# First stage of a streaming encoder step: low-rank columns on three 32-column strips, key products in another order, two value tiles ahead of the norm

## The chip, the core and the metric

The kernel runs on one core of a Trainium2 chip. The metric is the device time of one execution in microseconds (us). Engines are named as the profile names them: PE is TensorE, DVE is VectorE, ACT is ScalarE, POOL is GpSimd, SP is SyncE; PEld is TensorE's weight load, and a q behind a name (SPq, ACTq) is the issue of a DMA on that engine's queue.

## The reference, cut to what matters

The reference is one step of two layers over 1024 prompt frames and 64 sample frames of width 1024. The change lies in the beginning of the even layer, where the frames are normed and projected:

```python
h = _rmsnorm(x, norm_g)                       # x * rsqrt(mean(x*x) + eps) * g
z = h @ w_in
aq, ak, av, bq, bk, bv, blr, gate = _split(z, SPLIT_EVEN)
...                                           # ak, av: 256 columns each, blr: 16 columns
glog = jax.nn.log_sigmoid((blr @ w_lr + b_lr).astype(jnp.float32)) / B_GATE_NORM
```

The keys `ak` and values `av` go into sliding-window attention, `blr` gives the forget gates of four heads of gated linear attention. All is float32.

## The kernel before

Activations lie transposed, 8 blocks of 128 features by 1092 tokens (1024 + 64, padded), and a matmul takes a third of the tokens (364 columns; `NCH` = 3 of them). Weights come in pieces of 128x1024 in a fixed order: piece 0 the low-rank columns (16 real ones in a block of 128), 1 and 2 the keys (`PC_K`), 3 and 4 the values (`PC_V`), 5 and on the gates, queries and the rest. SP loads a piece into one of two slots of `raw`. POOL splits it by halves into a rounded high part `w_hi` (L343) and the remainder `w_lo` (L347); each half of a slot is free again when PE has used it. ACT makes the high part `H` of the inputs times the norm's gain (L771) and DVE the low part (L1111). A product is then three terms, high*high, low*high and high*low (`project`, L372), so nine matmuls for each block of 128 features, at the fast fp32r rate.

The norm's row factor is left out of `H` and put in afterwards: ACT squares each block of `X` into one buffer `sq` (L795), DVE adds it up in `acc` (L1146), PE sums over the partitions (`sum_squares`, L392), DVE and ACT form the inverse roots `rT` (L1123 to L1130) and a diagonal (L1133), PE broadcasts this (`broadcast`, L399 and L404), and ACT copies it to `rb` (L781). Keys and the low-rank rows are multiplied by `rb` on DVE, values by `rT` on ACT as they leave PSUM (L834).

PE's order is written out by hand: low-rank blocks 0 to 2, then low-rank and first key piece in turn, then the second key piece with `sum_squares` ahead of its block 2 and `broadcast` ahead of its block 6, then `project_v` (L418): nine tiles of 24 matmuls with 256 columns, tiles 0 and 1 interleaved, each later one waiting for its PSUM bank to be emptied by ACT. Then come the four pieces of the first gates and queries, and attention. The low-rank rows are used much later: `low_rank` (L526) multiplies them, per head, by a 16-row matrix padded to 128 rows; three float32 matmuls, each recorded as two instructions.

Of the kernel before, what the change touches and what calls it, by code (L numbers as in the profile page):

```python
# [65 lines left out]
USE_A = (2, 1)  # L66
# [55 lines left out]
def build_program(nc, xT, weights, vecs_d, consts_d, wlr_d, kc_d, vc_d, sg_d,  # L122
# [5 lines left out]
    with ctx:  # L128
# [58 lines left out]
        blr_raw = part(9 * TOK + NT * P, TOK)  # L187
        blrT = part(ARENA - 2 * TOK, TOK)
# [75 lines left out]
        bc_rest, rb_main = sem("bc_rest"), sem("rb_main")  # L264
        v_done, v_free = sem("v_done"), sem("v_free")
# [37 lines left out]
        def _(sp):  # L303
            sp.dma_start(raw[:, 0, :], weights[0]).then_inc(w_in[0], 16)
# [24 lines left out]
            load_run(2, PC_B0 + 1, queries_first)  # L329
# [6 lines left out]
        def _(pool):  # L336
            def split(i, s, first):
                pool.wait_ge(w_in[s], 16 * i + 16)
                for h in range(2):
# [3 lines left out]
                    pool.tensor_tensor(w_hi[:, s, cols].rearrange("p (k n) -> p k n", n=P),  # L343
                                       raw[:, s, cols].rearrange("p (k n) -> p k n", n=P), every_tile_ones,
                                       ALU.mult).then_inc(w_hi_done, 1)
                    pool.wait_ge(w_hi_done, 4 * i + (2 * s + h + 1))
                    pool.tensor_tensor(w_lo[:, s, cols], raw[:, s, cols], w_hi[:, s, cols].bitcast(F32),  # L347
# [5 lines left out]
            for s in range(2):  # L353
                split(0, s, True)
            with pool.Fori(1, PIECES // 2) as i:
                for s in range(2):
                    split(i, s, False)
# [3 lines left out]
        def _(pe):  # L361
# [25 lines left out]
            def sum_squares(n):  # L387

                pe.wait_ge(acc_done, KD * (n + 1))
                for t in range(NT):  # L390
                    m = TOK - SEQ if t == NT - 1 else P
                    mm = pe.matmul(ps[0:m, 7, t:t + 1], acc[:, t * P:t * P + m], ones[:, 0:1], start=True, stop=True)  # L392
                mm.then_inc(ssq_done, 1)

            def broadcast(n, bank):

                pe.wait_ge(diag_done, n + 1)
                for c in range(2):
                    mm = pe.matmul(ps[:, 6 + c, :], ones, diag[:, 4 * c:4 * c + 4, :].rearrange("p t n -> p (t n)"),  # L399
# [8 lines left out]
            def project_v(piece, base, between=None):  # L408
# [16 lines left out]
                for half in range(2):  # L425
                    for t in range(2):
                        v_tile(t, range(4 * half, 4 * half + 4))
                for t in range(2, NT):
# [8 lines left out]
            def low_rank_input(k):  # L437
                mm = project(0, [k], PC_LR, H_hi, H_lo, 0, first=(k == 0), last=(k == KD - 1), at0=k,
                             ready=(h_lo_done, 0))
                if k == KD - 1:  # L440
# [1290 lines left out]
```

## Time and profile before

| what | us |
|---|---|
| median of 3 runs | 1553.69 (1553.51 to 1554.33) |
| the profiled execution, its own time | 1548.58 |
| its span (first to last instruction) | 1546.8 |
| PE busy | 1483.7 (96%) |
| POOL busy | 703.5 (45%) |
| first matmul starts | 9.60 |
| first value tile starts | 58.86 |
| third value tile starts | 66.38 |
| first gate piece starts | 87.27 |

The profiled execution is read for places and durations; its own time stands 5.1 us under the median of the timed runs, so a difference worked out in it is applied to the median. In a timeline row the columns are start, duration (both us), engine, line, operation, what is written and read, and how many instructions the row merges; brackets give the idle time ahead of it and what ended it. A group of matmuls that follow on each other ends, in the records, about as late as its last result; the distance of starts is the rate.

### The profile page before, as it was taken

What the parts mean: (1) busy time and instruction counts of PE and PEld (TensorE: products, weight loads), DVE (VectorE), ACT (ScalarE), POOL (GpSimd) and SP (SyncE); (2) the same over time, 40 slices, a digit from 0 to 9 for tenths busy, and PEclk for the clock granted to TensorE, in tenths of its full rate; (3) what the DMA queues carried; (4) which work ended last, traced back from release to release, by engine and by line L of the source; (5) the groups of instructions that cost most, each with busy time, mean ns of one, the idle gap of its engine ahead of it and who ended that gap; (6) DMA issues with size and microseconds to landing.
All of it is one profiled execution on the core that took longest, in us unless ns stands there. A gap on an engine that the chain in (4) does not pass through costs nothing.

```text
span 1546.8 us, 23448 instructions
## 1 busy us (share of the span) xinstructions
PE 1483.7 (96%) x9332; PEld 1415.4 (92%) x9332; DVE 828.5 (54%) x1193; ACT 452.7 (29%) x766; POOL 703.5 (45%) x461
## 2 busy tenths in 40 slices
PE   6999999999999999999999999989999999989994
PEld 5999888887799989999889999989999999989993
DVE  7112655566645547245375111487888888881114
ACT  5111434345432220320141000325153351550000
POOL 5353222222123335223336444358577685766550
PEclk9999999999999999999999999999999999999996
DMA  4311111100010011110104223111111111123322
GB/s 187 108 52 38 31 55 28 44 28 15 30 33 35 33 34 41 46 34 31 35 28 142 72 86 109 43 55 47 50 55 55 42 55 55 43 70 97 97 70 116
DMA packets 27418, 89.80 MB, mean 58 GB/s; under 512 B 3600, under 2 KB 6736, under 8 KB 27344
## 3 DMA queue, kind: packets, MB, share of 16 engines
q1 hardware_dynamic: 16560, 60.34, 11.9%
q10 hardware_dynamic: 10784, 28.39, 5.6%
q8 instruction: 58, 0.95, 0.2%
q14 instruction: 16, 0.13, 0.0%
HBM read 77.16 MB, written 11.68 MB: 57 GB/s over the span
## 4 chain that ended last, share of the span: by engine, by line
PE 90%; DVE 4%; POOL 3%; issue 3%; DMA 0%; ACT 0%; ACTq 0%; POOLq 0%; DVEq 0%; SPq 0%
PE ps L372 57%; PE ps L542 11%; PE ps L418 7%; PE ps L481 2%; PE ps L515 2%; PE ps L502 2%; PE ps L703 2%; POOL w_hi L343 1%; POOL w_lo L347 1%; PE ps L618 1%; PE ps L602 1%; PE ps L613 1%; DVE arena L1607 1%; DVE arena L1146 1%; PE ps L594 1%
## 5 line engine op out<-in xcount | busy, mean ns | idle before, releaser
L343 POOL TENSOR_TENSOR w_hi<-raw,ones 128x512 fp32r<-128x512 f32 x228 | 344.5, 1511 | 789.5 <-PE ps L372 453.3
L372 PE MATMUL ps<-H,w_hi 128*128 128x364 f32 x2736 | 557.7, 331 | 27.7 <-DVE H L1111 15.2
L372 PEld LDWEIGHTS ps<-H,w_hi 128*128 128x128 f32 x2736 | 469.4, 189 | 32.1 <-issue 21.4
L372 PE MATMUL ps<-H,w_lo 128*128 128x364 f32 x1704 | 377.7, 330 | 0.0
L347 POOL TENSOR_TENSOR w_lo<-raw,w_hi 128x512 fp32r<-128x512 f32 x228 | 360.5, 1581 | 17.9
L372 PEld LDWEIGHTS ps<-H,w_lo 128*128 128x128 f32 x1704 | 298.6, 190 | 0.0
L372 PE MATMUL ps<-Yr,w_hi 128*128 128x364 f32 x672 | 149.3, 330 | 0.0
L542 PE MATMUL ps<-H,w_hi 128*128 128x364 f32 x672 | 144.2, 338 | 0.7 <-DVE Y L1237 0.7
L1464 DVE TENSOR_TENSOR arena<-ps,arena 128x1092 f32 (+1 forms) x16 | 20.7, 1296 | 219.2 <-PE ps L372 219.2
L418 PE MATMUL ps<-w_hi,H 128*128 128x256 f32 (+1 forms) x720 | 132.4, 284 | 2.9 <-ACT Y L834 1.2
L542 PEld LDWEIGHTS ps<-H,w_hi 128*128 128x128 f32 x672 | 111.7, 188 | 14.8 <-issue 10.9
L372 PEld LDWEIGHTS ps<-Yr,w_hi 128*128 128x128 f32 x672 | 117.9, 190 | 0.0
L418 PEld LDWEIGHTS ps<-w_hi,H 128*128 128x128 f32 (+1 forms) x720 | 110.1, 185 | 4.5 <-POOL w_lo L347 1.8
L874 ACT ACTIVATE arena<-arena,sm 128x256 f32<-128x256 f32 (+2 forms) x144 | 69.0, 481 | 133.9 <-DVE sm L1192 133.9
L418 PE MATMUL ps<-w_lo,H 128*128 128x256 f32 (+1 forms) x360 | 101.5, 282 | 0.0
L1025 ACT ACTIVATE arena<-arena 128x1092 f32<-128x1092 f32 x16 | 17.9, 1118 | 265.4 <-DVE arena L1464 254.3
L1192 DVE CUSTOM_DVE_ANT_0 arena<-ps,arena,nsink 128x256 f32<-128x256 f32 (+2 forms) x144 | 57.8, 456 | 59.7 <-PE ps L481 59.7
L542 PE MATMUL ps<-H,w_lo 128*128 128x364 f32 x336 | 74.8, 331 | 0.0
L372 PE MATMUL ps<-ur,w_hi 128*128 128x364 f32 x336 | 68.5, 334 | 5.1 <-issue 5.1
L418 PEld LDWEIGHTS ps<-w_lo,H 128*128 128x128 f32 (+1 forms) x360 | 66.5, 185 | 0.3
L1544 DVE SCALAR_TENSOR_TENSOR Y<-arena,cur,Y 128x1092 f32<-128x1092 f32 x36 | 65.9, 1830 | 1.3
L372 PEld LDWEIGHTS ps<-ur,w_hi 128*128 128x128 f32 x336 | 58.5, 192 | 5.4 <-issue 5.4
(182 smaller groups left out, 1726.9 us busy)
## 6 DMA issues: line engine op xcount, KB each, us to landing
raw<-weights SPq DMA_DIRECT2D x114, 512.0 KB, 3.5
arena<-xT ACTq DMA_DIRECT2D x15, 546.0 KB, 4.9
x_scratch<-arena ACTq DMA_DIRECT2D x8, 546.0 KB, 5.3
arena<-x_scratch ACTq DMA_DIRECT2D x8, 546.0 KB, 3.6
yT<-arena ACTq DMA_DIRECT2D x8, 546.0 KB, 3.1
arena<-k_scratch ACTq DMA_DIRECT2D x8, 304.0 KB, 4.8
k_scratch<-Y ACTq DMA_DIRECT2D x2, 512.0 KB, 2.7
arena<-xT SPq DMA_DIRECT2D x1, 546.0 KB, 5.1
```

Of the source, the lines that this page charges most:

```text
L343: pool.tensor_tensor(w_hi[:, s, cols].rearrange("p (k n) -> p k n", n=P), raw[:, s, cols].rearrange("p (k n) -> p k n", n=P), every_tile_ones,
L347: pool.tensor_tensor(w_lo[:, s, cols], raw[:, s, cols], w_hi[:, s, cols].bitcast(F32), ALU.subtract).then_inc(w_split, 1)
L372: mm = pe.matmul(sets[st][:, c, 0:CW], lw[:, s, w], rx[:, k, c * CW:(c + 1) * CW], start=(first and n == 0 and m == 0), stop=(last and n = ...
L418: mm = pe.matmul(ps[0:m, 6 + t % 2, 0:256], lx[:, k, t * P:t * P + m], rw[:, s, wk], start=(k == 0 and n == 0), stop=(k == KD - 1 and n == 2))
L481: mm = pe.matmul(ps[0:r, 3 + j, 2 * P * b + c0:2 * P * b + c0 + k1 - k0], q_of[g][rows, b, t * P:t * P + r], kz[rows, g % 2, k0:k1], start ...
L502: mm = pe.transpose(ps[0:rows, 5 + kt, at:at + r], Ssb[0:r, U % 3, 2 * b + j, kt * P:kt * P + rows], ident[0:r, 0:r])
L515: mm = pe.matmul(by_head(ps[64 * j:64 * j + 64, 7, 0:2 * P])[:, :, 0:r], V[0:rows, tile, A_DIM * g:A_DIM * (g + 1)], by_head(PT[0:rows, U ...
L542: mm = pe.matmul(sets[0][:, c, 0:CW], lw[:, 1 - n % 2, k * P:(k + 1) * P], rx[:, k, c * CW:(c + 1) * CW], start=(x == 0), stop=(x == 3 * K ...
L703: mm = pe.matmul(sets[n][:, c, 0:CW], lw[:, 1 - n, w], rx[:, k, c * CW:(c + 1) * CW], start=(k == 0 and m == 0), stop=(k == KD - 1 and m = ...
L874: act.activation(Ssb[0:r, r3, h, c0:c1], Ssb[0:r, r3, h, c0:c1], ACT.Exp, bias=sm[0:r, r3, 0, h:h + 1], scale=-1.0, accum_out=sm[0:r, r3, ...
L1192: dve.tensor_tensor_reduce(Ssb[0:r, r3, h, c0:c1], ps[0:r, 3 + j, 2 * P * b + c0:2 * P * b + c1], bt[0:r, g % 2, h, c0:c1], -float(A_DIM) ...
L1544: dve.scalar_tensor_tensor(U[:, n, :], xc[:, j:j + TOK], cur[:, n, j:j + 1], U[:, n, :], ALU.mult, ALU.add).then_inc(cv_step if j < 3 else ...
```

## The change

- **Low-rank columns.** They are no longer split. The weights of piece 0 go to a buffer of their own; POOL cuts 32 columns of them and multiplies these by the gain. PE multiplies them with `X` itself in float32, the three thirds of the tokens on three strips of 32 columns of the array: partitions 0 to 31, 32 to 63 and 64 to 95 of one PSUM bank. The result is 96x364 rather than 128x1092. `low_rank` then has strips too, of 32 rows each (three matmuls that read 32 partitions), and its small matrix is loaded three times.
- **Keys.** Both key pieces are split into buffers of their own, so that POOL can split the value pieces without waiting for PE. PE goes through low-rank block k and the two high-part terms of key piece 0, block k; then the two high-part terms of key piece 1; then the low-part terms of both.
- **Norm.** ACT does all eight high parts first and all eight squares afterwards, into eight buffers. DVE does all eight low parts ahead of the sums. `sum_squares` stands behind value tiles 0 and 1, `broadcast` behind tile 2.
- **ACT behind it.** The first key piece is copied from PSUM and scaled in place later. Value tiles 0 to 3 are copied ahead of the DMAs that write the keys out, the others behind them.
- SP loads `X` block 0 first, then the low-rank piece, then the two key pieces.

On PE, from the program's start. Before (`ps<-H,w_hi` is a product in PSUM from H and the high weights):

```order
L372 MATMUL ps<-H,w_hi 128x364 [waits h_lo_done,w_split,ones_set]
L372 MATMUL ps<-H,w_hi 128x364 x2
L372 MATMUL ps<-H,w_lo 128x364 x3
L372 MATMUL ps<-H,w_hi 128x364 x3
L372 MATMUL ps<-H,w_hi 128x364 [waits h_lo_done]
```

And now (`arena` is X, `Y` the narrow low-rank weights, `Yr` the split key weights):

```order
L463 MATMUL ps<-arena,Y 32x364 [waits w_split,x_in0,ones_set]
L463 MATMUL ps<-arena,Y 32x364 x2
L477 MATMUL ps<-H,Yr 128x364 [waits h_hi_done,w_split]
L477 MATMUL ps<-H,Yr 128x364 x5
L463 MATMUL ps<-arena,Y 32x364 [waits x_in1]
```

Each block now has three narrow float32 matmuls and six wide ones, waits for DVE's low parts have left this stretch, and the first key block waits for POOL.

On PE, around `sum_squares`. Before, it stands within the second key piece:

```order
L372 MATMUL ps<-H,w_hi 128x364 x3
L392 MATMUL ps<-ones,arena 128x1 [waits acc_done]
L392 MATMUL ps<-ones,arena 128x1 x7
L392 MATMUL ps<-ones,arena 68x1
L372 MATMUL ps<-H,w_hi 128x364 x3
```

Now it stands between value tile 1 and value tile 2, which waits for ACT's copy of tile 0:

```order
L436 MATMUL ps<-w_hi,H 128x256
L410 MATMUL ps<-ones,arena 128x1 [waits acc_done,drained1]
L410 MATMUL ps<-ones,arena 128x1 x7
L410 MATMUL ps<-ones,arena 68x1
L436 MATMUL ps<-w_hi,H 128x256 [waits v_free]
```

The copy of tile 0 needs `rT`, so the inverse roots now lie directly ahead of tile 2.

On POOL, the first splits. Before:

```order
L343 TENSOR_TENSOR w_hi<-raw,ones 128x512 [waits w_in0,ones_set]
L347 TENSOR_TENSOR w_lo<-raw,w_hi 128x512 [waits w_hi_done]
L343 TENSOR_TENSOR w_hi<-raw,ones 128x512
L347 TENSOR_TENSOR w_lo<-raw,w_hi 128x512 [waits w_hi_done]
L343 TENSOR_TENSOR w_hi<-raw,ones 128x512 [waits w_in1]
```

And now:

```order
L366 TENSOR_TENSOR Y<-Y,vecs 128x128 [waits lr_in,vecs_in,ones_set]
L366 TENSOR_TENSOR Y<-Y,vecs 128x128
L351 TENSOR_TENSOR Yr<-raw,ones 128x512 [waits w_in1]
L355 TENSOR_TENSOR Yr<-raw,Yr 128x512 [waits w_hi_done]
L351 TENSOR_TENSOR Yr<-raw,ones 128x512
```

The key pieces' splits have no wait for PE, nor have those of the two value pieces behind them; the first with such a wait is piece 5.

The diff, cut to its core:

```diff
             sp.dma_start(X[:, 0, :], xT[0]).then_inc(x_in[0], 16)
+            sp.dma_start(lr_raw.rearrange("p k n -> p (k n)"), weights[0]).then_inc(lr_in, 16)
             sp.dma_start(raw[:, 1, :], weights[1]).then_inc(w_in[1], 16)
+            sp.dma_start(raw[:, 0, :], weights[2]).then_inc(w_in[0], 16)
...
             def low_rank_input(k):
-                mm = project(0, [k], PC_LR, H_hi, H_lo, 0, first=(k == 0), last=(k == KD - 1), at0=k,
-                             ready=(h_lo_done, 0))
...
+                for c in range(NCH):
+                    mm = pe.matmul(ps[32 * c:32 * c + 32, 6, 0:CW], w_lr[:, k, :], X[:, k, c * CW:(c + 1) * CW],
+                                   start=(k == 0), stop=(k == KD - 1))
...
+            for k in K8:
                 low_rank_input(k)
+                keys(0, k, (0, 1))
             for k in K8:
...
+                keys(1, k, (0, 1))
+            for n in range(2):
+                for k in K8:
+                    keys(n, k, (2,))
+            pe.wait_ge(blr_copied, 1)
...
+            project_v(PC_V, 0, lambda: broadcast(0, 3, 4), first_sums)
...
             def low_rank(h, before):
...
+                    rows = slice(32 * c, 32 * c + 32)
+                    mm = pe.matmul(sets[0][:, c, 0:CW], wlr_cur[rows, :], blrT[rows, :],
                                    start=True, stop=True)
...
+            for b in range(KD):
+                act.activation(sq_of[:, b, :], X[:, b, :], ACT.Square).then_inc(sq_done, 1)
...
+            act.wait_ge(rt_done, 1)
+            for t in range(2):
+                first_values(t)
+            norm_copy(0, 3)
+            for t in range(2, 4):
+                first_values(t)
+            for b in range(2):
+                act.wait_ge(*((k_ready, 1), (drained[0], 1))[b])
...
+            dve.wait_ge(sq_done, 2)
+            dve.tensor_tensor(acc, sq_of[:, 0, :], sq_of[:, 1, :], ALU.add).then_inc(acc_done, 2)
```

## Rows read from the trace of the kernel before

**Rows 1.** The page: busy time by engine, and the chain that ended last.
```profile
PE 1483.7 (96%) x9332; PEld 1415.4 (92%) x9332; DVE 828.5 (54%) x1193; ACT 452.7 (29%) x766; POOL 703.5 (45%) x461
...
PE 90%; DVE 4%; POOL 3%; issue 3%; DMA 0%; ACT 0%; ACTq 0%; POOLq 0%; DVEq 0%; SPq 0%
```

**Rows 2.** Timeline of PE, 0 to 60 us: start, duration, what.
```profile
9.60 1.25 PE L372 MATMUL ps<-H,w_hi 128*128 128x364 f32 x3 [9.60 <-DVE H L1111]
...
15.16 1.11 PE L372 MATMUL ps<-H,w_lo 128*128 128x364 f32 x3
...
18.66 0.78 PE L372 MATMUL ps<-H,w_hi 128*128 128x364 f32 x3 [1.48 <-DVE H L1111]
...
46.01 1.96 PE L392 MATMUL ps<-ones,arena 128*128 128x1 f32 x18
47.84 0.75 PE L372 MATMUL ps<-H,w_hi 128*128 128x364 f32 x3
...
53.93 1.88 PE L399 MATMUL ps<-arena,ones 128*128 128x512 f32 x4
...
55.79 0.75 PE L372 MATMUL ps<-H,w_hi 128*128 128x364 f32 x3
...
58.86 0.28 PE L418 MATMUL ps<-w_hi,H 128*128 128x256 f32 x1
```

**Rows 3.** Timeline of DVE, same stretch.
```profile
11.66 2.37 DVE L1111 SCALAR_TENSOR_TENSOR H<-arena,vecs,H 128x1092 fp32r<-128x1092 f32 x1
...
34.35 1.30 DVE L1146 TENSOR_TENSOR arena<-arena 128x1092 f32<-128x1092 f32 x1
...
48.95 1.36 DVE L1133 TENSOR_TENSOR arena<-consts,rT 128x1152 f32<-128x1152 f32 x1
```

**Rows 4.** Timeline of POOL, same stretch.
```profile
10.54 2.33 POOL L343 TENSOR_TENSOR w_hi<-raw,ones 128x512 fp32r<-128x512 f32 x1
12.95 2.21 POOL L347 TENSOR_TENSOR w_lo<-raw,w_hi 128x512 fp32r<-128x512 f32 x1
...
37.28 1.30 POOL L343 TENSOR_TENSOR w_hi<-raw,ones 128x512 fp32r<-128x512 f32 x1 [9.10 <-PE ps L372]
```

**Rows 5.** Timeline of SP: the issue of the second weight piece.
```profile
1.67 0.42 SPq L306 DMA_DIRECT2D raw<-weights  x1
```

**Rows 6.** DMA issues, 1.65 to 2 us: count, size, median us to landing.
```profile
raw<-weights SPq DMA_DIRECT2D x1, 512.0 KB, 7.8
```

**Rows 7.** Timeline of PE, 133 to 160 us (attention; 64-row and 64-column tiles).
```profile
143.04 0.66 PE L542 MATMUL ps<-H,w_hi 128*128 128x364 f32 x3
143.63 1.13 PE L481 MATMUL ps<-arena,Y 64*128 64x256 f32 x8
144.69 0.77 PE L542 MATMUL ps<-H,w_hi 128*128 128x364 f32 x3
145.30 0.66 PE L542 MATMUL ps<-H,w_lo 128*128 128x364 f32 x3
...
152.40 0.65 PE L515 MATMUL ps<-arena,Y 128*64 128x256 f32 x4
152.98 0.77 PE L542 MATMUL ps<-H,w_hi 128*128 128x364 f32 x3
```

**Rows 8.** The chain that ended last, 405 to 430 us: start, duration, what.
```profile
412.00 2.07 PE ps L526 x6
...
427.38 1.83 PE ps L526 x6
```

**Rows 9.** Timeline of DVE, 408 to 418 us.
```profile
412.15 1.89 DVE L1212 TENSOR_TENSOR arena<-arena,sm 64x768 f32<-64x768 f32 x1
```

**Rows 10.** Timeline of PE, first matmul of value tile 2.
```profile
66.38 0.38 PE L418 MATMUL ps<-w_hi,H 128*128 128x256 f32 x1 [1.22 <-ACT Y L834]
```

**Rows 11.** Timeline of ACT, copies of value tiles 2 and 3.
```profile
69.51 0.47 ACT L834 ACTIVATE Y<-ps,rT 128x256 f32<-128x256 f32 x1 [2.82 <-PE ps L418]
72.34 0.47 ACT L834 ACTIVATE Y<-ps,rT 128x256 f32<-128x256 f32 x1 [2.36 <-PE ps L418]
```

More of the change, by code:

```diff
@@ L336, in _, with split @@
         def _(pool):
-            def split(i, s, first):
-                pool.wait_ge(w_in[s], 16 * i + 16)
+            def split(i, s, first, hi=None, lo=None):
+                hi, lo = w_hi[:, s, :] if hi is None else hi, w_lo[:, s, :] if lo is None else lo
+                pool.wait_ge(w_in[s], 16 * i + 16 * s)
                 for h in range(2):
@@ new lines, in low_rank_input, with keys @@
+                if k % 4 == 3:
+                    mm.then_inc((half_done, piece_done)[k // 4], 1)
+            def keys(n, k, ms):
+                pe.wait_ge(w_split, 2 * (PC_K + n) + k // 4 + 1)
+                pe.wait_ge(h_hi_done, k + 1)
+                if 2 in ms:
+                    pe.wait_ge(h_lo_done, k + 1)
+                w = slice(k * P, (k + 1) * P)
+                for m in ms:
+                    lw, rx = ((wk_hi, H_hi), (wk_lo, H_hi), (wk_hi, H_lo))[m]
+                    for c in range(NCH):
+                        mm = pe.matmul(sets[1 - n][:, c, 0:CW], lw[:, n, w], rx[:, k, c * CW:(c + 1) * CW],
+                                       start=(k == 0 and m == 0), stop=(k == KD - 1 and m == 2))
+                if 2 in ms and k % 4 == 3:
+                    mm.then_inc((half_done, piece_done)[k // 4], 1)
@@ L780, in norm_copy @@
                 act.wait_ge(bc_done, n + 1)
-                main = act.activation(rb[:, 0:SEQ].rearrange("p (a n) -> p a n", a=2), ps[:, 6:8, :], ACT.Copy)
+                at = 6 if n else 4
+                main = act.activation(rb[:, 0:SEQ].rearrange("p (a n) -> p a n", a=2), ps[:, at:at + 2, :], ACT.Copy)
                 if bank is None:
@@ L820, in bias_table @@
                 last.then_inc(bt_ready, 1)
+            for t in range(4, NT):
+                first_values(t)
             act.wait_ge(k_all_in, 80)
@@ L826, in _ @@
             load_keys(1)
-            act.wait_ge(rt_done, 1)
-            for t in range(NT):
-                r = tile_rows(t)
-                if t < NT - 1:
-                    act.wait_ge(v_done, t + 1)
-                else:
-                    act.wait_ge(piece_done, PC_V + 2)
-                act.activation(V[0:r, t if t < 8 else 9, :], ps[0:r, 6 + t % 2, 0:256], ACT.Copy,
-                               scale=rT[0:r, t:t + 1]).then_inc(v_free, 1)
             act.wait_ge(v_free, NT)
@@ L846, in _, with load_low_rank @@
                 gate_tanh_of(n, USE_A[n] + 1)
+            def load_low_rank(src):
+                for c in range(NCH):
+                    act.dma_start(wlr_cur[32 * c:32 * c + 32, :], src[0:32, :]).then_inc(wlr_in, 16)
             def gate_bias(h):
```

122 lines of the change are left out of this document (67 added, 55 removed).

## The prediction

> **What bounds the kernel now.** I read the page first, the chain that ended last second, and then the timelines of the first 90 us. PE is busy 96% of the span and carries 90% of the chain [rows 1], so matmul time that is removed, or an idle stretch of PE that closes, comes off the total unless something else is late right behind it. The reader should then look at the start. PE's first matmul comes at 9.60, released by DVE's low part of block 0. It goes on with gaps of about 1.5 us, each ended by another low part [rows 2]. Three wide matmuls take 1.11 us at 15.16, which is the pace of the lower clock level (364 columns in about 0.3 us, 1.2 GHz). From 18.66 they take two thirds of that and less, the pace of 2.4 GHz. Later 36 of them go from 47.84 to 53.93: 0.169 us each. The first value tile starts at 58.86. Of the time to there, 1.83 us are the sums (46.01 to 47.84) and 1.86 us the broadcast (53.93 to 55.79) [rows 2], so keys and low-rank columns are done after 55.2 us, of which their 216 matmuls make 216 * 0.169 = 36.5 and waiting and the slow clock 18.7. Behind them, value tile 2 starts at 66.38 after 1.22 us of idleness [rows 10]. I use that start as the mark: beyond it both kernels run the same value tiles, except for the broadcast.
>
> **When the new order can start.** The low-rank blocks need only X and narrow weights, but PE's queue is in order, and behind low-rank block 0 stands key block 0, which waits for POOL's first half of the key piece. That piece is the third DMA on SP's queue, as the second weight piece was before, behind nearly the same bytes: issued at 1.67 [rows 5], landed 7.8 us later [rows 6], so at 9.5. POOL then needs a high and a low part. While DVE works with two SBUF inputs both engines are slow: POOL's pair is 2.33 and 2.21 [rows 4], DVE's low part 2.37 [rows 3]; alone, one is 1.30 on either side. DVE will have low parts to do all through this (X arrives faster than DVE does them), so I take 4.6 us: keys start at **14.1**. The bound on the other side is an undisturbed POOL, 2 * 1.3, and 12.1. The two small multiplications of POOL ahead of it fit into the wait for the DMA, and low-rank block 0 too.
>
> **What PE does from there.** Two key pieces are 2 * 8 * 9 = 144 wide matmuls, as before: 144 * 0.169 = 24.3. Seven low-rank blocks are left; call one of them with all its switching x. Before, a block was nine wide matmuls, 1.5 us. Now it is six narrow instructions in float32. The trace has no 32-column strip; the nearest rows are these. The float32 product of three thirds in `low_rank` takes 1.83 us for six instructions in a row [rows 8], 0.305 each. Tiles on different halves of the array run beside each other: the four instructions of two 64-column tiles last 0.65 us [rows 7]. In a row they would take 4 * 256 columns at that float32 rate (0.213 each), 0.85, and about 0.24 of latency (2.07 less 1.83 [rows 8]), 1.09 in all; side by side 0.43 + 0.24 = 0.67. Three strips side by side are then 2 * 0.305 = 0.61. Switching costs on top: the wide group of 143.04 should free PE at 143.55, and the one of 144.69 gets to its second three at 145.30, which without a switch would be a start at 144.79. Of these 1.24 us the eight row-tiled instructions need 4 * 0.213 = 0.85 side by side, so an excursion costs 0.39 [rows 7]. That gives **x = 1.0**, an estimate from two tiles carried to three; its bounds are 1.0 and, with strips in a row, 1.83 + 0.39 = 2.2. I take the lower end since both tiled rows that the trace has, by rows and by columns, show tiles fully side by side.
>
> The Trainium skill (TensorEngine Tiling (Array Packing), Key Properties) says that different tiles can load weights and run matmuls in parallel, but also that a change of tiling mode drains TensorE. The second speaks against this change, which changes mode sixteen times in the first stage. The 0.39 us per excursion in rows 7 agrees with a drain, and it is in x; by the page alone it would have no price.
>
> The clock: PE idles from about 8 to 14 and starts slow again. Before, it took until 18.66 with gaps in the work. I let the slow pace last to 18.5 and charge half of 4.4 us, **2.2** (bounds 1 and 4).
>
> No other wait ends later, by my sum. X and H arrive ahead of their block: ACT needs 8 blocks at about 1.2 us, PE takes 2. POOL at the slow rate needs 2.3 us a step: key piece 0 is split at 18.7, piece 1 at 27.9, value piece 3 at 37, value piece 4 by about 45. The first is needed at about 24 (block 4), the second at 31 to 35, the third at 47.8 and the fourth at 50.6. DVE has low parts until 26 (needed from 39) and the seven adds until 42, where the sums stand at 53.5. If this cover is gone by some us, the value pieces are the first to be late.
>
> So keys and low-rank end at 14.1 + 24.3 + 7x + 2.2 = 47.6. Value tiles 0 and 1 take 2 * 2.83 = 5.7 (the distance of tiles is 72.34 - 69.51 [rows 11]): 53.3. The sums take 1.8: 55.1.
>
> **The wait that is added.** Behind the sums PE stands at tile 2 until ACT has copied tile 0, for which it needs the inverse roots. From the sums' last result at 47.97 to the start of the diagonal, which follows the roots, at 48.95 are 0.98 us [rows 2, 3]; with the copy of 0.47 [rows 11] and hand-overs some 1.6 us with the last result's latency. Nothing hides it; it stands in the place of the 1.22 us that PE waits there now [rows 10]. Tile 2 starts at **56.7**, and before at 66.38: 9.7 us earlier. The broadcast, which lay ahead of that mark, now follows it, 1.9 us: **7.8 us** are left of the first stage. The diagonal (1.36 [rows 3]) is ready within tile 2. ACT's two broadcast copies (1.25 together) and its copy of tile 2 end within tile 3. Next, ACT issues six DMAs for the keys in front of the copy of tile 4, some 3.5 us after the first scaled key piece. Tile 6 wants that copy about 5.7 us after tile 4 has begun; I find 0.2 us to spare and charge nothing, at most 1 us if DVE's in-place scaling is slowed. Later stages hide the moved DMAs, since scores begin only at 136.8. At the end of the value tiles POOL waits for PE and PE for POOL as before.
>
> **low_rank, four times.** The one at 412.00 saves nothing: the transposes behind it need DVE's normalisation, which runs from 412.15 for 1.89 us [rows 9], to 414.04, when before they start at 414.19. The other three stand in unbroken PE work (1.83 each [rows 8]) and become x: 3 * (1.83 - 1.0) = **2.5 us**. ACT's two more DMA issues per head stand ahead of one activation with a tile of slack.
>
> **The sum.** As a function of x, the change is -7.8 - 7(1.0 - x) - 3(1.83 - x) = 10x - 20.3 us; at x = 1.0 it is **-10.3**. From the profiled execution, 1548.6, that is 1538.3; applied to the median, 1553.7 - 10.3 = **1543.4**, 0.66% faster. The measurement can tell about 0.2%, 3.1 us, from no change; so faster means x below 1.72, slower x above 2.34.
>
> **Rivals.**
> - Early start: POOL is not slowed at 9.5, or the switches are cheaper than in rows 7. Two us better, 1541.4. Against it: every POOL step beside DVE's low parts takes above 2.2.
> - Half overlap: a strip's second instruction holds up the next strip, so four steps of 0.305 pass in place of two: x = 1.22 + 0.39 = 1.6, change -4.3, 1549.4. For it: in-order issue. Against it: 0.65 us for four instructions in rows 7.
> - No overlap (the change doesn't do what it says): x = 2.2, change +1.7, 1555.4, no measurable change. For it: nothing here shows 32-column strips or three of them.
> - No overlap, and both switches of an excursion expose the array's latency once more, 2 * 0.24: x = 2.7, +6.7, 1560.4, **slower**. The narrow steps are ten excursions on the path; it decides for slower from x = 2.34. For it: the drain rule above, with short groups of six instructions. Against it: rows 7 have the same kind of switch at 0.39.
>
> **Chances.** The forecast with its early variant has 0.72 (early 0.12 of it), half overlap 0.12, no overlap 0.10, slower 0.06. The range holds the first two and what their unknown costs make of them (start 12.1 to 14.1, clock 1 to 4, tile 6 up to 1): 1540.5 to 1550. Faster 0.83, within 0.2% 0.11, slower 0.06.
>
> **What would show it.** Right: a row for the narrow matmuls whose six instructions last about 0.85 us, with starts 2.0 us apart from block to block; the first key matmul at 14.1, released by POOL's low part; the low-part terms done at 47.6; tile 2 at 56.7 after some 1.6 us of idleness ended by ACT; `low_rank` rows of about 0.85 us in the head loop. Wrong: key matmuls that wait on POOL again within the first piece, a slow pace that lasts beyond 20 us, value tiles 0 or 1 waiting for POOL's value pieces, or the sums waiting for the adds on DVE.

## Result, and the profile after

| | before | after |
|---|---|---|
| timed beside each other, median | 1553.6 (4 executions, 1548.53 to 1554.33) | 1538.32 (4 executions, 1536.99 to 1539.56) |
| all executions of this study, mean | 1551.1 (89, 1545.05 to 1556.72) | 1540.7 (19, 1536.99 to 1546.79) |
| the profiled execution, its own time | 1548.58 | 1538.98 |
| its span | 1546.8 | 1537.2 |
| first gate piece starts | 87.27 | 79.83 |

The ratio of the first comparison is 0.9912 [0.9891, 0.9932]: 0.9% faster. The forecast was 1543.4 in a range of 1540.5 to 1550, so the time lies below the range. The change itself was forecast at -10.3 us. Between the two profiled executions it is -9.6, and between the means of all executions -10.4 (95%: -12.0 to -8.6). These means pool several chips and sessions; within the sessions that timed both kernels, the means differ by -14.2, -11.2 and -9.6. The difference was forecast within this uncertainty and the absolute time was not; the experiments had to find out why.

The page of after: busy time of each engine, its share and its number of instructions. It answers to [rows 1].

```profile
PE 1477.2 (96%) x9308; PEld 1403.1 (91%) x9308; DVE 836.9 (54%) x1193; ACT 452.9 (29%) x767; POOL 703.5 (46%) x459
```

PE still bounds the kernel. Its busy time fell by 6.5 us and its idle time by 3.1, together the 9.6 of the span.

The timeline of PE in after, 7 to 62 us (start, duration, what; in brackets the idle time ahead and its releaser). It answers to [rows 2, 10].

```profile
7.08 1.44 PE L463 MATMUL ps<-arena,Y 128*32 128x364 f32 x6 [7.08 <-POOL Y L366]
...
13.09 2.19 PE L477 MATMUL ps<-H,Yr 128*128 128x364 f32 x6 [4.57 <-POOL Yr L355]
...
16.57 2.19 PE L477 MATMUL ps<-H,Yr 128*128 128x364 f32 x6
18.69 0.90 PE L463 MATMUL ps<-arena,Y 128*32 128x364 f32 x6
...
22.66 0.81 PE L463 MATMUL ps<-arena,Y 128*32 128x364 f32 x6
...
24.61 0.81 PE L463 MATMUL ps<-arena,Y 128*32 128x364 f32 x6
...
46.28 0.28 PE L436 MATMUL ps<-w_hi,H 128*128 128x256 f32 x1
...
51.97 1.96 PE L410 MATMUL ps<-ones,arena 128*128 128x1 f32 x18
...
55.44 0.38 PE L436 MATMUL ps<-w_hi,H 128*128 128x256 f32 x1 [1.50 <-ACT Y L849]
...
57.12 0.63 PE L436 MATMUL ps<-w_hi,H 128*128 128x256 f32 x2
...
59.89 1.88 PE L417 MATMUL ps<-arena,ones 128*128 128x512 f32 x4
...
61.75 0.37 PE L436 MATMUL ps<-w_hi,H 128*128 128x256 f32 x1
```

- Keys start at 13.09, a microsecond ahead of the forecast 14.1.
- Blocks of the first key piece are 24.61 - 22.66 = 1.95 us apart. Six wide matmuls take 6 * 0.169 = 1.01 of that, which leaves 0.94 for a low-rank step with its switches (forecast 1.0).
- The row at 16.57 has six wide matmuls at 0.3 us and more each, the pace of 1.2 GHz; at 18.69 that is over, as forecast (18.5). The profile's granted clock reads 1.00 from 13.0 to 18.7 all the same, so here the pace is read from the distance of the starts.
- The first value tile starts at 46.28 (47.6), value tile 2 at 55.44 after 1.50 us of idleness ended by ACT (56.7 after 1.6).
- Tile 2 itself takes 59.89 - 55.44 = 4.45 us, where a tile takes 2.83 at full pace. This was in no step of the forecast.

PE in windows of after (stretch, length, busy time and count of PE, PEld, DVE, ACT, POOL, granted clock, share of DMA time, GB/s): keys and values up to the sums, then tile 2.

```profile
46.00:52.00 6.00, 6.00 (x53) 6.00 (x51) 0.00 (x0) 0.00 (x0) 0.00 (x0) 1.00 0.17 68
55.40:59.90 4.50, 4.46 (x25) 4.46 (x26) 0.95 (x2) 0.35 (x1) 0.00 (x0) 0.62 0.08 25
```

In the six microseconds ahead of the sums PE had the full clock. Behind the sums' eighteen one-column instructions and 1.50 us of idleness it was granted 0.62 on the mean until the end of tile 2. For about a microsecond its matmuls start 0.12 us apart, and from 56.5 on 0.21, the pace of 1.2 GHz for 256 columns. That cost 4.45 - 2.83 = 1.6 us. The six other traces that have the sums in this place show 4.19 to 5.29 us for tile 2. In [rows 2] the sums stood between wide matmuls with no idle time behind them, and the 1.22 us of idleness ahead of tile 2 in before [rows 10] followed wide matmuls: there the copy of tile 3 came 2.83 us after that of tile 2 [rows 11], which is full pace. Whether the single columns or the length of the idleness makes this difference, no run separates.

The timeline of POOL in after: the first key piece, and the first split that waits for PE's last value tile.

```profile
9.49 1.27 POOL L351 TENSOR_TENSOR Yr<-raw,ones 128x512 fp32r<-128x512 f32 x1 [2.19 <-DMA raw<-weights]
10.83 2.20 POOL L355 TENSOR_TENSOR Yr<-raw,Yr 128x512 fp32r<-128x512 f32 x1
...
77.05 1.29 POOL L351 TENSOR_TENSOR w_hi<-raw,ones 128x512 fp32r<-128x512 f32 x1 [32.73 <-PE ps L436]
```

The timeline of DVE in after, the low part that meets the first split:

```profile
9.81 2.09 DVE L1162 SCALAR_TENSOR_TENSOR H<-arena,vecs,H 128x1092 fp32r<-128x1092 f32 x1 [1.37 <-ACT H L809]
```

Weights landed at 9.5 as forecast; the high part took 1.27 and not 2.3, because it began while DVE was still waiting for an X block. DVE joined it at 9.81 and then took 2.09 us for its own instruction. POOL's last row above starts at 84.49 in before: the first stage is 7.44 us shorter (forecast 7.8). Other traces scatter around this: the first gate piece starts at 88.25, 88.02 and 86.70 in three further traces of before and at 79.39 and 79.05 in two of after. The Trainium skill (GPSIMD Engine Reference, Specifications) says that GpSimd contends with DVE instructions that have two SBUF inputs; 1.27 for the instruction that began beside an idle DVE (which paid instead) and 2.20 for the one that began beside a busy one agree with it.

The timeline of PE in after at `low_rank`, first and second head, and then a window from the one to the other, in after and in before (there it ends 0.2 us short of the second). They answer to [rows 8].

```profile
404.56 0.89 PE L564 MATMUL ps<-arena,wlr_cur 32*128 32x364 f32 x6 [0.22 <-DVE Y L1293]
...
406.74 0.65 PE L539 MATMUL ps<-consts,arena 64*128 64x64 f32 x8 [1.30 <-DVE arena L1268]
...
420.96 0.89 PE L564 MATMUL ps<-arena,wlr_cur 32*128 32x364 f32 x6
```

```profile
404.50:420.90 16.40, 13.61 (x94) 12.13 (x94) 8.73 (x27) 8.44 (x10) 1.27 (x1) 0.79 0.11 36
```

```profile
412.00:427.00 15.00, 13.45 (x93) 11.86 (x94) 8.69 (x27) 8.08 (x10) 1.24 (x1) 0.89 0.13 40
```

The six instructions took 2.07 us and now take 0.89, and PE waits 1.30 for DVE instead: this one gives nothing, as forecast. Between the first and the second `low_rank` are 16.4 us where before had 427.22 - 412.00 = 15.2, with a granted clock of 0.79 against 0.89. The other heads are in unbroken work: from the second to the third, 518.38 - 420.96 = 97.42 against 525.46 - 427.22 = 98.24, so 0.82 us each (forecast 0.83).

Behind the last head both kernels have the same row of PE, and nothing that the change touches follows it. Before, then after:

```profile
739.67 0.46 PE L589 MATMUL ps<-arena 128*128 128x128 f32 x2 [0.65 <-ACT arena L930]
...
730.90 0.46 PE L627 MATMUL ps<-arena 128*128 128x128 f32 x2 [0.65 <-ACT arena L983]
```

So 8.8 of the 9.6 us come from the places that were changed; the other 0.8 arose where the two programs are alike.

### The profile page after: what moved, and what is told of

It reads as the page before. It is cut to its first block, busy times and chain, and to the rows that moved or that the text cites. A ratio compares the mean times of both kernels' runs of the same rounds, so it can differ in the third digit from the quotient of the medians.

```text
span 1537.2 us, 23430 instructions
## 1 busy us (share of the span) xinstructions
PE 1477.2 (96%) x9308; PEld 1403.1 (91%) x9308; DVE 836.9 (54%) x1193; ACT 452.9 (29%) x767; POOL 703.5 (46%) x459
## 4 chain that ended last, share of the span: by engine, by line
PE 94%; DVE 3%; POOL 1%; issue 1%; DMA 1%; ACT 0%; SPq 0%; DVEq 0%; POOLq 0%; ACTq 0%
PE ps L390 59%; PE ps L580 11%; PE ps L436 8%; PE ps L518 2%; PE ps L552 2%; PE ps L539 2%; PE ps L477 2%; PE ps L741 2%; PE ps L656 1%; PE ps L640 1%; PE ps L651 1%; DVE arena L1663 1%; PE ps L632 1%; PE ps L627 1%; PE ps L629 1%
## 5 line engine op out<-in xcount | busy, mean ns | idle before, releaser
L351 POOL TENSOR_TENSOR w_hi<-raw,ones 128x512 fp32r<-128x512 f32 x222 | 335.0, 1509 | 772.8 <-PE ps L390 428.3
L390 PE MATMUL ps<-H,w_hi 128*128 128x364 f32 x2592 | 526.3, 330 | 12.5 <-DVE Yr L1572 6.0
L390 PEld LDWEIGHTS ps<-H,w_hi 128*128 128x128 f32 x2592 | 443.7, 188 | 15.4 <-issue 11.8
L390 PE MATMUL ps<-H,w_lo 128*128 128x364 f32 x1632 | 360.8, 329 | 0.0
L355 POOL TENSOR_TENSOR w_lo<-raw,w_hi 128x512 fp32r<-128x512 f32 x222 | 352.2, 1586 | 17.4
L390 PEld LDWEIGHTS ps<-H,w_lo 128*128 128x128 f32 x1632 | 285.2, 189 | 0.0
L580 PE MATMUL ps<-H,w_hi 128*128 128x364 f32 x672 | 144.2, 338 | 0.7 <-DVE Y L1293 0.7
L580 PEld LDWEIGHTS ps<-H,w_hi 128*128 128x128 f32 x672 | 111.7, 188 | 14.8 <-issue 10.9
L580 PE MATMUL ps<-H,w_lo 128*128 128x364 f32 x336 | 74.8, 331 | 0.0
```

The source lines that it names most:

```text
L351: pool.tensor_tensor(hi[:, cols].rearrange("p (k n) -> p k n", n=P), raw[:, s, cols].rearrange("p (k n) -> p k n", n=P), every_tile_ones, ...
L355: pool.tensor_tensor(lo[:, cols], raw[:, s, cols], hi[:, cols].bitcast(F32), ALU.subtract).then_inc(w_split, 1)
L390: mm = pe.matmul(sets[st][:, c, 0:CW], lw[:, s, w], rx[:, k, c * CW:(c + 1) * CW], start=(first and n == 0 and m == 0), stop=(last and n = ...
L580: mm = pe.matmul(sets[0][:, c, 0:CW], lw[:, 1 - n % 2, k * P:(k + 1) * P], rx[:, k, c * CW:(c + 1) * CW], start=(x == 0), stop=(x == 3 * K ...
```

## The experiments

Two questions were open. The first was whether the terms of the sum were right one by one: the narrow step x, its half in `low_rank`, the order of the key terms, and what the sums' place costs. The second was where the 5 us between the forecast and the result came from: a gain that the sum lacks, or the base to which it was applied. All ratios are against before, timed in the same session on the same chip. Where executions scatter, means are used beside them; the 1540.7 of after pools its 19 executions of three sessions, with a standard deviation of 3.5 us, so a difference of two such means is good to about 2 us either way.

### Before and after once more

`before_again`, the kernel before, without an edit.

> The kernel before, unchanged, timed against itself. In the comparison the changed kernel is 0.88% faster (13.7 us of 1552), while the spans of the two profiled executions differ by 9.6 us only, close to the 10.3 of my sum. Theory one: the kernel before has executions near 1548.5 and others near 1553.7, for a reason that its profiled execution (1548.6) does not have, and the sum is right for the former. Then several rounds show values near both 1548.5 and 1553.7. Theory two: its time is 1553.7 on any chip and the profiled one was a rare execution; then all rounds lie within 1 us of 1553.7 and the change removes some 4 us that the trace of before did not contain.

Measured: 12 executions from 1545.97 to 1555.89, median 1550.75, ratio 0.9996 [0.9979, 1.0014]; the 25 executions of before that stood beside them have 1546.19 to 1556.72 and a median of 1551.64. The same program thus spreads over 11 us. The 1553.69 from which the forecast was taken, with a range of 0.8 us, was the middle of three close draws from this: 34 of all 89 executions are at 1553 or above, and the quartiles are 1548.3, 1551.1 and 1554.4. The base was 2.6 us above the mean.

`after_again`, the changed kernel without an edit.

> The changed kernel, unchanged. If the difference is stable, the ratio is 0.991 with an interval within 0.989 to 0.993; if the runs of before spread over two levels, a ratio between 0.991 and 0.994, and this kernel's own runs within 1537 to 1540.

Measured: 1537.47, 1538.08, 1538.19, 1538.95, 1540.23 and 1546.78, ratio 0.9930 [0.9903, 0.9957]. After has an upper part too, and the four executions of the result had missed it.

`after_third`, again without an edit.

> The changed kernel again, to know its spread: of ten executions nine lay at 1537 to 1540.2 and one at 1546.8. If it has the two groups too, 1 to 3 of 12 lie near 1547 and its lower group stands 9.5 us under the lower group of before (1547.5), which is what the two traces and my sum say.

Measured: nine executions, 1537.06 to 1546.79, median 1540.77, four of them above 1544; ratio 0.9944 [0.9921, 0.9967]. Over its 19 executions after has a mean of 1540.7, 2.4 above the mean of the first four. So one half of the miss is the base of before (2.6), the other the lucky first four of after (2.4). Chips may play a part as well, since after's sessions have means of 1538.3, 1540.0 and 1542.3; no run tells them from the scatter.

### The narrow products

`one_strip`: the three products of a low-rank block stand on one strip and no longer on three.

```diff
                 for c in range(NCH):
-                    mm = pe.matmul(ps[32 * c:32 * c + 32, 6, 0:CW], w_lr[:, k, :], X[:, k, c * CW:(c + 1) * CW],
-                                   start=(k == 0), stop=(k == KD - 1))
+                    s = k % 3 if k else c
+                    mm = pe.matmul(ps[32 * s:32 * s + 32, 6, 0:CW], w_lr[:, k, :], X[:, k, s * CW:(s + 1) * CW],
+                                   start=(k == 0), stop=(k >= KD - 3 and c == NCH - 1))
```

> The changed kernel with the three low-rank products of one block on one and the same 32-column strip, so that none can lie beside another; the low-rank values are not the ones wanted (each strip gets three times its own third for some blocks and none for others), the count and form of matmuls is the same. If the strips run side by side, a step grows from the 0.74 us that the trace of the changed kernel shows to about 6 * 0.305 + 0.1 = 1.95, and the seven steps on the path cost 7 * 1.2 = 8.5 us more, 1547. If the array serialises them anyway, nothing changes.

The timeline of PE in `one_strip`, two low-rank blocks and value tile 2:

```profile
19.87 2.02 PE L464 MATMUL ps<-arena,Y 128*32 128x364 f32 x6
...
23.00 2.02 PE L464 MATMUL ps<-arena,Y 128*32 128x364 f32 x6
...
63.73 0.58 PE L436 MATMUL ps<-w_hi,H 128*128 128x256 f32 x1 [1.50 <-ACT Y L850]
```

A row takes 2.02 instead of 0.81, the distance of blocks is 3.13 instead of 1.95, and tile 2 starts 63.73 - 55.44 = 8.3 us later. In time, the mean of 12 executions (1542.39 to 1559.47) is 1549.4, 8.7 above after; ratio 0.9989 [0.9963, 1.0014]. Three strips do run fully side by side, and without that the change brings almost nothing. The third rival (x = 2.2, change +1.7) was right about its price and wrong about the chip: here the change is -1.7, and `low_rank` in the heads, which still has its three tiles, would add the 3.5 of the next run.

`heads_one_tile`: the three products of `low_rank` stand on one tile of 32 rows.

```diff
-                    rows = slice(32 * c, 32 * c + 32)
+                    rows = slice(0, 32)
```

> The changed kernel with all three matmuls of low_rank in the four heads on the first 32-row tile (the forget gates of the second and third part of the tokens are then those of the first), so that they cannot lie beside each other. With three tiles the six instructions last 0.89 us in the trace of the changed kernel, and took 2.00 before. Theory: the narrower rows alone save nothing, tiles side by side do; then the six last about 2.0 us again and the three heads in unbroken PE work give back 3 * 1.1 = 3.3 us. Rival: 32-row matmuls are short by themselves; then the row stays near 0.9.

The timeline of PE in `heads_one_tile`, second and third head:

```profile
418.06 2.10 PE L564 MATMUL ps<-arena,wlr_cur 32*128 32x364 f32 x6
...
516.66 2.10 PE L564 MATMUL ps<-arena,wlr_cur 32*128 32x364 f32 x6
```

2.10 against 0.89, and 98.60 us from head to head against 97.42: 1.18 for each of three heads, 3.5 in all. The mean of 12 executions is 1544.6, 3.9 above after; ratio 0.9963 [0.9942, 0.9985].

This run also tells something of the first head. Its six instructions take 2.07 us again, the wait of 1.30 behind them is gone, and the second head follows 418.06 - 402.76 = 15.30 us after the first. The five traces of kernels with `low_rank` in its old form have 13.7 to 15.2 there; all eight with three tiles have 16.1 to 16.5. So at the first head the shorter row costs time, about 1 to 2.8 us.

### The order of the key terms, and the place of the sums

`block_order`: PE does all three key terms of a block before it goes to the next, as before the change.

```diff
             for k in K8:
                 low_rank_input(k)
-                keys(0, k, (0, 1))
+                keys(0, k, (0, 1, 2))
             for k in K8:
-                keys(1, k, (0, 1))
-            for n in range(2):
-                for k in K8:
-                    keys(n, k, (2,))
+                keys(1, k, (0, 1, 2))
```

> The changed kernel with the three terms of a key product in one go, block by block, as before the change; everything else as changed. It tells what 'high parts first' is worth. By my sum PE needs 0.74 + 9 * 0.167 = 2.24 us a block and DVE brings a low part every 2.2 us from 8.4 on, three blocks ahead of PE; then nothing is lost and the value tiles start at 46.3 as in the changed kernel, total within 1 us. Rival: the low parts are late in the first blocks (the first three of them are done at 8.4, 11.9 and 14.9 in the trace) or the pieces' second halves are; then PE waits and the value tiles start up to 4 us later.

The timeline of PE in `block_order`, value tile 2:

```profile
55.31 0.38 PE L436 MATMUL ps<-w_hi,H 128*128 128x256 f32 x1 [1.50 <-ACT Y L846]
```

Tile 2 starts at 55.31 against 55.44, and the mean of 12 executions is 1540.4 against 1540.7; ratio 0.9942 [0.992, 0.9963]. The new order of the key terms is worth nothing in the trace, and nothing that the times can tell. With three terms to a block PE still waits for nothing between 13.04 and the first value tile: its step of 2.4 us is long enough for DVE's low part (2.3).

`sums_in_keys`: the sums go back into the second key piece, ahead of the low-part term of its block 2, into a bank of their own. The broadcast stays where it was, behind value tile 2.

```diff
             for n in range(2):
                 for k in K8:
+                    if (n, k) == (1, 2):
+                        sum_squares(0)
                     keys(n, k, (2,))
             pe.wait_ge(blr_copied, 1)
+            pe.wait_ge(ms_done, 1)
 
-            def first_sums():
+            def first_broadcast():
                 pe.wait_ge(drained[1], 1)
-                sum_squares(0, 3)
+                broadcast(0, 3, 4)
 
-            project_v(PC_V, 0, lambda: broadcast(0, 3, 4), first_sums)
+            project_v(PC_V, 0, first_broadcast)
...
-                bank = 7 if n else 3
+                bank = 7
```

> The changed kernel with sum_squares put back into the key products (ahead of the low-part term of key piece 1, block 2, in PSUM bank 7), the broadcast left ahead of value tile 3. In the changed kernel PE idles 1.50 us ahead of value tile 2 and that tile's matmuls then run at the slow pace (tile 2 and what stands ahead of the broadcast take 4.45 us in place of 2.83). Theory: both come from the place of the sums. Then tile 2 starts without idleness, no matmul of tiles 0 to 3 is at the slow pace, and the kernel is 1.5 + 1.6 = 3.1 us faster than the changed one, near 1535. Rival: the slow pace there has another cause; then only the 1.5 us come, near 1537. Second rival: the adds on DVE, done at 41.8, are late for PE and the sums wait.

`sums_in_keys_again` is the same kernel, without a further edit.

> The version with the sums back among the key products, again: its eight executions were five at 1532.3 to 1535.6 and three at 1543.9 to 1546.6. By its trace the first stage is 3.35 us shorter than in the changed kernel. If that holds, its lower group is at 1534 to 1535.5, its ratio to before stays near 0.991, and the upper group appears in about 1 of 3.

The timeline of PE in `sums_in_keys_again`: sums, broadcast, first gate piece.

```profile
43.22 1.97 PE L410 MATMUL ps<-ones,arena 128*128 128x1 f32 x18
...
56.64 1.88 PE L417 MATMUL ps<-arena,ones 128*128 128x512 f32 x4
...
76.55 0.74 PE L390 MATMUL ps<-H,w_hi 128*128 128x364 f32 x3 [0.83 <-POOL w_lo L355]
```

The sums stand at 43.22 between wide matmuls, nothing waits behind them, tile 2 runs at full pace, and the first gate piece starts at 76.55 against 79.83 in after. Those 3.3 us are, but for 0.2, the idle time of 1.50 and the slow pace of 1.6 that after pays for its place of the sums. In time it is not settled. The two comparisons have ratios of 0.9914 [0.9887, 0.9941] and 0.9913 [0.9882, 0.9945]; 15 executions have a mean of 1538.1 (1532.29 to 1547.59) against after's 1540.7, a difference of -2.6 with a 95% interval of -5.6 to +0.6. The lowest execution of the study, 1532.29, is of this kernel, but its upper part lies as high as after's.

The profiled execution of `sums_in_keys` is such an upper one (span 1544.6). A window in its second head, and the same in after (columns as above):

```profile
440.00:462.00 22.00, 21.32 (x135) 19.32 (x135) 14.44 (x44) 6.74 (x11) 4.02 (x4) 0.92 0.18 61
```

```profile
440.00:462.00 22.00, 21.32 (x147) 18.82 (x147) 12.67 (x37) 4.58 (x11) 7.20 (x6) 1.00 0.18 61
```

PE is busy for as long and does fewer instructions, at a granted clock of 0.92. The same dip comes in three heads (1.5 us each); waits for DVE of 0.23 and 3.14 behind 796 us, with a slow pace after them, come on top. Some 2 to 3 us of that execution's excess between 709 and 1520 us I could not account for.

The profiled execution of `one_strip`, at 1554.25, lies 11.9 above the lowest of its kernel and has the same dips: 98.97 and 98.96 us from head to head where after has 97.42 and 97.44. `after_third`'s trace has them in two heads (98.97 in the first of them), and the traces of before have none.

### What the scatter comes from

`after_again` shows a wait of 3.14 us for DVE near 810 us that after and before have not. The timeline of PE in `after_again`:

```profile
796.61 0.77 PE L390 MATMUL ps<-H,w_hi 128*128 128x364 f32 x3 [0.23 <-DVE Yr L1386]
...
810.52 1.28 PE L390 MATMUL ps<-H,w_hi 128*128 128x364 f32 x3 [3.14 <-DVE Yr L1386]
```

My theory then was that this race between PE and DVE divides the executions. It was tested by giving PE 12 more matmuls (about 2 us) in front of that place, in both kernels, of which nothing reads the result.

`more_pe_work_after` is after with this edit:

```diff
                             for k in range(3):
                                 out_tile(0, kt, half, k, piece, ready)
+                            if base == PC_OE and not half:
+                                for x in range(12):
+                                    pe.matmul(ps[:, 6, 0:CW], w_hi[:, 1, 0:P], H[:, 0, 0:CW], start=True, stop=True)
```

> The changed kernel with 12 more matmuls of 364 columns (about 2.0 us) whose result nobody reads, behind the first three blocks of the even layer's output projection, at about 784 us. In two executions of the changed kernel a slow pace of PE at 783 us delays it by 1.9 us and no wait comes after it; where the pace stays fast, POOL's split at 786 falls beside DVE's subtractions, both are slowed, and PE waits 0.23 and 3.14 us later, at 796 and 810, part of it with a slow clock behind. Theory: this hand-over is what spreads the runs; then the added 2 us remove the wait of 3.1 us, the time is not above that of the changed kernel (1538.5) but within 1 us of it. Rival: the wait does not hang on PE's lateness and the kernel is 2 us slower, 1540.5.

`more_pe_work_before` is before with the same three lines:

```diff
+                            if base == PC_OE and not half:
+                                for x in range(12):
+                                    pe.matmul(ps[:, 6, 0:CW], w_hi[:, 1, 0:P], H[:, 0, 0:CW], start=True, stop=True)
```

> The same 12 matmuls in the kernel before. Its 37 executions so far lie between 1546 and 1557, its two traces (1547.5 and 1548.6) both have the slow pace at 793 and no wait of 3.1 us behind it. Theory: the executions above 1551 are those in which the pace stays fast there and the wait comes; then the added work takes them away, the spread shrinks and the median falls from 1551.6 to about 1549 or below. Rival: the spread comes from other places; then the median rises by 2, to 1553.6, with the same spread.

Measured: after with more work has eight executions from 1538.17 to 1541.68, mean 1539.9; ratio 0.9936 [0.9912, 0.9959]. Before with more work has 12 from 1546.51 to 1555.33, mean 1549.9; ratio 1.0001 [0.9982, 1.002]. Only one of these 20 is in the upper part (of before 34 of 89, of after 5 of 19), and both means are no higher than without the 2 us of work. With so few executions that is a hint, not a proof, that the place matters. The trace of `more_pe_work_after` has no wait for DVE there, but this on POOL:

```profile
801.88 9.69 POOL L351 TENSOR_TENSOR w_hi<-raw,ones 128x512 fp32r<-128x512 f32 x1 [9.25 <-PE ps L390]
```

A split that takes 1.3 us alone and 2.3 beside DVE took 9.69, and PE then waited 1.81 us for POOL. The trace of `more_pe_work_before` has the same, 9.68 and 1.80, at 1549.64. Neither is an upper execution. That was the trail.

`before_third` and `before_fourth` are the kernel before again, profiled once each.

> The kernel before once more, for its trace. The executions of before lie in a lower group (1545 to 1550) and an upper one (1554 to 1557); both traces so far are of the lower. In an execution of the upper group (chance about 1 in 3) the theory of a shifting slow pace expects, against the trace of the lower group: 2 to 5 us more within the three passes of the head loop (412 to 717), with a granted clock under 1.00 in each, and a wait of about 3.1 us on DVE in the output projection's first pair. In one of the lower group nothing new.

> As before_third: one more trace of the kernel before, to see where an execution of the upper group loses its time.

`before_third` took 1549.38 and has the very waits of `after_again`, 0.23 at 805.21 and 3.14 at 819.12, yet is no upper execution. Nor is `after_again`'s own trace, at 1540.23. So the wait for DVE does not by itself divide the executions.

`before_fourth` took 1554.42, `before_again`'s trace 1547.54: 6.9 us between two executions of one program. At 716 us both are at the same place (716.08 and 716.26). Their timelines of POOL and of DVE from 807 us on, `before_fourth` first:

```profile
808.05 11.71 POOL L343 TENSOR_TENSOR w_hi<-raw,ones 128x512 fp32r<-128x512 f32 x1 [9.22 <-PE ps L372]
...
808.87 2.48 DVE L1409 SCALAR_TENSOR_TENSOR Y<-Y,arena 128x1092 f32<-128x1092 f32 x2
811.28 7.31 DVE L1330 TENSOR_TENSOR Yr<-Y,H 128x1092 fp32r<-128x1092 f32 x6
```

Then `before_again`:

```profile
808.24 2.02 POOL L343 TENSOR_TENSOR w_hi<-raw,ones 128x512 fp32r<-128x512 f32 x1 [9.24 <-PE ps L372]
810.34 2.23 POOL L347 TENSOR_TENSOR w_lo<-raw,w_hi 128x512 fp32r<-128x512 f32 x1
...
809.03 4.69 DVE L1409 SCALAR_TENSOR_TENSOR Y<-Y,arena 128x1092 f32<-128x1092 f32 x2
813.64 13.91 DVE L1330 TENSOR_TENSOR Yr<-Y,H 128x1092 fp32r<-128x1092 f32 x6
```

The same instructions meet at the same time. In one execution both engines are slowed alike, DVE to 2.3 us an instruction and POOL to 2.2. In the other DVE runs at full speed, 7.31 us for six, and POOL's one split stands for 11.71 us; it ends 1.2 us after DVE is done with them. PE needs POOL's halves. The timeline of PE in `before_fourth`:

```profile
823.74 1.28 PE L372 MATMUL ps<-H,w_hi 128*128 128x364 f32 x3 [3.79 <-POOL w_lo L347]
824.82 1.11 PE L372 MATMUL ps<-H,w_lo 128*128 128x364 f32 x3
```

And the window around it, `before_fourth` and then `before_again`:

```profile
812.00:832.00 20.00, 16.21 (x83) 15.91 (x82) 11.28 (x12) 4.61 (x7) 16.56 (x8) 0.83 0.31 109
```

```profile
812.00:832.00 20.00, 20.00 (x122) 19.96 (x122) 17.19 (x13) 5.22 (x7) 14.17 (x7) 1.00 0.32 109
```

122 matmuls in one, 83 in the other. The 39 that are missing are 39 * 0.169 = 6.6 us, of 6.9 in all: 3.8 of waiting and the rest the slow pace behind it. This one upper execution is explained.

All traces can be cut at the same marks: the row of PE behind the last head (shown above for before and after), and POOL's first and last split of 3.3 us. In before these are:

```profile
1048.99 3.30 POOL L347 TENSOR_TENSOR w_lo<-raw,w_hi 128x512 fp32r<-128x512 f32 x1
...
1366.59 3.29 POOL L347 TENSOR_TENSOR w_lo<-raw,w_hi 128x512 fp32r<-128x512 f32 x1
```

| trace | its own time | to the end of the heads | from there to POOL's first 3.3 | from POOL's last 3.3 to the end |
|---|---|---|---|---|
| `before` | 1548.58 | 739.7 | 309.3 | 180.2 |
| `before_again` | 1547.54 | 739.1 | 308.8 | 180.2 |
| `before_third` | 1549.38 | 739.0 | 312.6 | 178.4 |
| `before_fourth` | 1554.42 | 738.9 | 315.9 | 180.2 |
| `after` | 1538.98 | 730.9 | 309.0 | 179.6 |
| `after_again` | 1540.23 | 730.4 | 312.6 | 177.9 |
| `after_third` | 1539.46 | 733.0 | 309.1 | 178.0 |
| `sums_in_keys_again` | 1535.53 | 727.5 | 309.0 | 179.6 |
| `sums_in_keys` | 1546.39 | 732.3 | 314.7 | 180.0 |

The stretch that is left out, between the two splits, is 317.6 us in every one. Between these traces the scatter is mostly a sum of separate steps: the dips in the heads (1.5 us each), the wait for DVE (3.5 with what follows it) or POOL's long split (6.9), and 1.8 us near the end, whose cause stays open. `before_third` pays for the wait and gets half of it back near the end; the two upper executions in the table do not get it back.

That the other upper executions of before have the cause of `before_fourth` is inferred and not shown: the three executions that set the base left no trace. No upper execution of after was profiled either, and those of `sums_in_keys` and `one_strip` have the dips and no split above 3.3 us. So the long split is one cause of several.

## Why the prediction was right, and where it was wrong

**The step that failed** is the last one of the sum: "applied to the median, 1553.7 - 10.3". The three executions lay within 0.8 us of each other, and I took them for the level of the kernel, though the profiled execution of the same program stood 5.1 us under them. That gap was a sign of the scatter, and I read it as an offset between profiled and timed executions. Applied to the profiled execution, the same -10.3 gives 1538.3, where its counterpart has 1538.98. With the mean of before, 1551.1 - 10.3 = 1540.8, where after's mean is 1540.7. That these agree to 0.1 us is luck, as the interval of the difference is 3.4 us wide and the traces show only 8.8 us at the places that were changed. The result's own four executions lie another 2.4 us lower, which no step of the prediction could know. The range held the unknown costs and left out the scatter of executions: a standard deviation of 3.5 us on either side, some 2 us for a median of three or four. It would have had to reach about 3 us further down, to 1537 or 1538.

**The terms of the sum**, forecast and measured:

| term | forecast | measured |
|---|---|---|
| keys start | 14.1 | 13.09 |
| one low-rank step with switches | 1.0 | 0.94 |
| slow pace lasts until | 18.5 | 18.7 |
| the slow pace costs | 2.2 | 2.3 (46.28 - 13.09 - 24.3 - 7 * 0.94) |
| first value tile | 47.6 | 46.28 |
| wait added behind the sums | 1.6 | 1.50 |
| tile 2 starts | 56.7 | 55.44 |
| tile 2 takes | 2.83 | 4.45 |
| first stage in all | -7.8 | -7.44 |
| tile 6, the wait for ACT's copy | 0 to 1 | none |
| `low_rank` at the first head | 0 | 0 at the row, +1.2 behind it |
| `low_rank`, each further head | -0.83 | -0.82 |
| all of these, at the end of the heads | -10.3 | -8.8 |

- The keys' start was mis-sized. I charged two contended POOL steps, and one of them began beside an idle DVE. That was the early rival, at half its size.
- x was right, and with it the choice among the rivals: `one_strip` shows what the no-overlap rival costs, and `heads_one_tile` the same for rows. The 0.39 of switching came out of an attention row with 64-wide tiles [rows 7] and carried over. The drain at a change of tiling mode that the Trainium skill states (TensorEngine Tiling (Array Packing), Key Properties) is thus small here: 1.95 - 1.01 - 0.61 leaves 0.33 us for the two switches around a low-rank step. The slower rival, which put the switches at 0.39 + 0.48 = 0.87, had no support.
- The wait behind the sums was forecast at the right size and without its sequel. The granted clock of 0.62 in tile 2 doubles its price, 1.50 + 1.6. It took back what the early start had given, so the stage came out near the forecast for two errors that cancel.
- The same sequel stands behind the first `low_rank`, 16.4 against 15.2 us to the next (13.7 in `before_again`). "Saves nothing" was too kind: it costs about 1 to 2.8, and `heads_one_tile`, where the row is long again and the wait of 1.30 gone, gives about 1.1 of it back.
- That the value pieces, the adds and the moved DMAs would find cover held: no row of PE waits for them. The keys' new order, which I had not priced apart, is worth nothing.

## What to carry to other kernels

Before a difference is added to a base, ask how far executions of the same program lie apart: here a profiled execution that disagreed with the timed ones was a sample of that spread, and no offset. Price a new wait of PE with what the clock does behind it, which here was as much as the wait. Small products that read the same input go on strips side by side, since the switch cost a third of a microsecond here. A sum of single columns had better stand in the middle of wide matmuls: in the trace that was worth 3.3 us, though the times do not settle it.

## What the runs showed of the hardware that I had not expected

- POOL's split beside DVE's instructions with two SBUF inputs had two outcomes in the same program: 2.0 to 2.4 us with DVE slowed to 2.3, or 11.71 us with DVE at 1.22. Between two executions this made 6.9 us.
- Three strips of 32 columns in float32 ran fully side by side, 0.81 us for six instructions against 2.02 on one strip; three tiles of 32 rows take 0.89 against 2.10.
- 1.50 us of idleness behind eighteen one-column matmuls were followed by 4.5 us at a granted clock of 0.62.
- A shorter group of matmuls in front of a wait cost time: 0.89 in place of 2.07 us at the first head, and 16.1 to 16.5 in place of 13.7 to 15.3 us to the next.
- Executions of a program on one core alone spread over 11 us, 0.7%, with a standard deviation of 3.5.
